# Wide U products in a sparse expert layer: one moving operand of 512 columns, and a sum of two PSUM halves on the vector engine

## The reference

```python
gate = jax.nn.softmax(best, axis=-1)
u = u_tab[idx]
h = jax.nn.gelu(jnp.einsum('bthkd,btd->bthk', u, xi).astype(jnp.float32), approximate=False)
w = (gate * h).astype(xi.dtype)
return jnp.einsum('bthk,bthkd->btd', w, v_tab[idx])
```

## Time and profile before

| | |
|---|---|
| time, median of 3 runs (lowest to highest) | 2306.07 us (2303.71 to 2306.95) |
| profiled execution, its own time | 2305.3 us |
| its span, first to last instruction | 2303.6 us |
| mean granted TensorE clock | 0.99 |
| PE busy | 2247.2 us, 98% of the span |
| DVE busy | 1399.5 us, 61% |
| ACT busy | 1241.2 us, 54% |
| POOL busy | 704.2 us, 31% |
| mean transfer rate | 163 GB/s |

### The profile page before, as it was taken

How to read it: one execution, slowest core, us unless ns; L and a number is a source line. 1 busy time by engine, 2 the same in 40 slices (tenths; PEclk the granted TensorE clock), 3 DMA queues, 4 the chain that set the end, 5 groups by cost and what they waited for, 6 DMA issues and landing times. The chain is left out here.

```text
span 2303.6 us, 38838 instructions
## 1 busy us (share of the span) xinstructions
PE 2247.2 (98%) x15059; PEld 2028.6 (88%) x15059; DVE 1399.5 (61%) x2682; ACT 1241.2 (54%) x2451; POOL 704.2 (31%) x346
## 2 busy tenths in 40 slices
PE   8799999999999999998999999999999999989999
PEld 7689999999888888886999999988888888888998
DVE  6546965566555555564697566655555558346555
ACT  4434467777544444464446777754444444545443
POOL 3205877777200000001487777720000004000000
PEclk9889999999999999999999999999999999999999
DMA  5125555555566666563565555566666656324654
GB/s 165 55 67 164 184 175 165 157 164 159 180 187 188 186 189 186 149 179 99 160 183 175 165 159 163 158 180 185 188 187 190 185 163 223 98 83 157 187 187 147
DMA packets 122535, 375.55 MB, mean 163 GB/s; under 512 B 13024, under 2 KB 17376, under 8 KB 122352
## 3 DMA queue, kind: packets, MB, share of 16 engines
q1 hardware_dynamic: 122352, 373.06, 53.0%
HBM read 371.96 MB, written 1.05 MB: 162 GB/s over the span
## 5 line engine op out<-in xcount | busy, mean ns | idle before, releaser
L248 ACT ACTIVATE hi<-raw 128x1024 fp32r<-128x1024 f32 (+1 forms) x703 | 737.2, 1050 | 429.8 <-PE bank L1249 184.5
L257 DVE TENSOR_TENSOR lo<-raw,hi 128x1024 fp32r<-128x1024 f32 (+2 forms) x443 | 536.9, 1215 | 372.4 <-ACT hi L248 372.0
L257 POOL TENSOR_TENSOR lo<-raw,hi 128x1024 fp32r<-128x1024 f32 x260 | 630.6, 2429 | 252.8 <-ACT hi L248 252.8
L1245 PE MATMUL bank<-xh,hi 128*128 128x256 f32 x2048 | 512.3, 288 | 0.0
L1246 PE MATMUL bank<-xl,hi 128*128 128x256 f32 x2048 | 500.8, 283 | 0.0
L1285 PE MATMUL bank<-hi,pe_mh 128*128 128x512 f32 x1016 | 403.3, 397 | 1.1 <-DVE pe_ml L1528 1.1
L1286 PE MATMUL bank<-hi,pe_ml 128*128 128x512 f32 x1016 | 402.8, 396 | 0.0
L1246 PEld LDWEIGHTS bank<-xl,hi 128*128 128x128 f32 x2048 | 391.8, 191 | 0.1
L1245 PEld LDWEIGHTS bank<-xh,hi 128*128 128x128 f32 x2048 | 390.8, 191 | 0.1
L320 POOL TENSOR_TENSOR rstd<-mean,minus_half 128x1 f32<-128x1 f32 x10 | 5.6, 556 | 976.6 <-DVE mean L327 976.6
L1396 ACT ACTIVATE pe_mh<-pe_hidden 128x256 fp32r<-128x256 f32 x256 | 107.0, 418 | 364.7 <-PE bank L1292 364.7
(11 more groups left out here) (395 smaller groups left out, 3237.7 us busy)
## 6 DMA issues: line engine op xcount, KB each, us to landing
raw<-in_peer_u SPq DMA_DIRECT2D x256, 512.0 KB, 3.6
raw<-in_peer_v SPq DMA_DIRECT2D x256, 512.0 KB, 4.1
raw<-in_w_gate_up SPq DMA_DIRECT2D x44, 512.0 KB, 4.2
raw<-in_w_in SPq DMA_DIRECT2D x34, 512.0 KB, 4.0
raw<-in_gla_w_in SPq DMA_DIRECT2D x24, 512.0 KB, 3.8
raw<-in_w_down SPq DMA_DIRECT2D x22, 512.0 KB, 4.2
raw<-in_w_query SPq DMA_DIRECT2D x16, 512.0 KB, 3.7
raw<-in_mla_w_o SPq DMA_DIRECT2D x8, 512.0 KB, 3.6
```

What stands on the lines that cost most here:

```text
L248: act.activation(k.hi[:, n % RING, 0:x * e], k.raw[:, n % RAW, 0:x * e], ACT.Copy).then_inc(k.hi_done, 1)
L257: eng.tensor_tensor(k.lo[:, n % RING, 0:x * e], k.raw[:, n % RAW, 0:x * e], k.hi[:, n % RING, 0:x * e].bitcast(F32), ALU.subtract).then_in ...
L1245: pe.matmul(ps, hi[:, r, c * P:(c + 1) * P], k.xh[:, c], start=(c == 0), stop=False)
```

## The change

The two activation tensors become one, `xx`, in which the high and the low 256 columns of each piece of the contraction lie side by side; `xh` and `xl` are views of it. From slab 44 on a U slab takes 7 matmuls of 512 columns (high part of the slab by both halves), then the 8 of 256 columns with the low part, and the eighth of 512 last. The bank's left half then holds what was multiplied with `xh`, its right half what was multiplied with `xl`. A new step on DVE, `fold(i)`, adds the two halves into `whole`, a new SBUF tile with two slots. `bend(i)` waits for `fold(i)` and works on `whole`, and `gate_slab(i)` multiplies with `whole`, where it multiplied with the PSUM bank before. PE waits for `folded` of slab i-3 before it writes the bank again.

```diff
-        self.xh = self.sb(ctx, "xh", [P, KD, T], F32R)
-        self.xl = self.sb(ctx, "xl", [P, KD, T], F32R)
+        self.xx = self.sb(ctx, "xx", [P, KD, 2, T], F32R)
+        self.xh, self.xl = self.xx[:, :, 0], self.xx[:, :, 1]
...
-                        if j > LEAD:
-                            pe.wait_ge(gated.sem, gated_before(j))
+                        if j >= LEAD:
+                            pe.wait_ge(folded.sem, folded.at(j - LEAD + 1))
...
-                    for c in range(KD):
-                        pe.matmul(ps, hi[:, r, c * P:(c + 1) * P], k.xh[:, c], start=(c == 0), stop=False)
-                        pe.matmul(ps, hi[:, r, c * P:(c + 1) * P], k.xl[:, c], start=False, stop=False)
+                    if i >= LEAD:
+                        for c in range(KD - 1):
+                            pe.matmul(k.bank[i % 3][:], hi[:, r, c * P:(c + 1) * P],
+                                      k.xx[:, c].rearrange("p s t -> p (s t)"), start=(c == 0), stop=False,
+                                      skip_group_check=True)
+                    else:
+                        for c in range(KD):
+                            pe.matmul(ps, hi[:, r, c * P:(c + 1) * P], k.xh[:, c], start=(c == 0), stop=False)
+                            pe.matmul(ps, hi[:, r, c * P:(c + 1) * P], k.xl[:, c], start=False, stop=False)
...
+                    if i >= LEAD:
+                        last = pe.matmul(k.bank[i % 3][:], hi[:, r, (KD - 1) * P:KD * P],
+                                         k.xx[:, KD - 1].rearrange("p s t -> p (s t)"), start=False, stop=True,
+                                         skip_group_check=True)
                     last.then_inc(k.eaten, 1)
...
-                    act.wait_ge(k.eaten, u0 + i + 1)
+                    if i >= LEAD:
+                        act.wait_ge(folded.sem, folded.at(i - LEAD + 1))
+                    else:
+                        act.wait_ge(k.eaten, u0 + i + 1)
                     ps, cut = first_ps(i), g * GROUP
+                    if i >= LEAD:
+                        ps = whole[:, i % 2]
...
+                def fold(i):
+
+                    dve.wait_ge(k.eaten, u0 + i + 1)
+                    if i >= LEAD + 3:
+                        dve.wait_ge(gated.sem, gated_before(i - 2))
+                    dve.tensor_reduce(whole[:, i % 2], k.bank[i % 3][:].rearrange("p (s t) -> p t s", s=2), AX_X, ALU.add)\
+                       .then_inc(folded.sem, 1)
...
-                    dve.tensor_tensor(hidden[:, i, 0:cut], hidden[:, i, 0:cut], first_ps(i)[:, 0:cut], ALU.mult)\
+                    dve.tensor_tensor(hidden[:, i, 0:cut], hidden[:, i, 0:cut], whole[:, i % 2, 0:cut], ALU.mult)\
                         .then_inc(gated.sem, 1)
...
                 for i in range(LEAD, NK):
+                    fold(i)
```

More of the change, by code:

```diff
@@ L283, in given_squares @@
         k = self.k
-        act.activation(k.xh[:, 0:4].rearrange("p c t -> p (c t)"), k.h[:, 0], ACT.Square, scale=D ** -0.5,
+        act.activation(k.xx[:, 0:2].rearrange("p c s t -> p (c s t)"), k.h[:, 0], ACT.Square, scale=D ** -0.5,
                        accum_out=k.mean[:, 0:1]).then_inc(self.squared.sem, 1)
@@ L296, in given_diagonals @@
         dve.tensor_tensor_reduce(
-            out=k.xl[:, 0:4].rearrange("p c t -> p (c t)"), in0=k.h[:, 1], in1=k.h[:, 1], scale=1.0 / D, scalar=0.0,
+            out=k.xx[:, 2:4].rearrange("p c s t -> p (c s t)"), in0=k.h[:, 1], in1=k.h[:, 1], scale=1.0 / D, scalar=0.0,
             op0=ALU.mult, op1=ALU.add, accum_out=k.mean[:, 1:2]).then_inc(self.summed.sem, 1)
@@ L1132, in peer @@
     names = ("q_act", "q_dve", "zeroed", "keyed", "scored", "s_act", "s_dve", "counted", "raised", "powered",
-             "ranked", "turned", "equal", "hotted", "lowered", "summed", "spread", "applied", "bent", "gated", "m_hi", "m_lo")
+             "ranked", "turned", "equal", "hotted", "lowered", "summed", "spread", "applied", "bent", "gated", "m_hi", "m_lo", "folded")
     (q_act, q_dve, zeroed, keyed, scored, s_act, s_dve, counted, raised, powered, ranked, turned, equal, hotted,
-     lowered, summed, spread, applied, bent, gated, m_hi, m_lo) = (k.sig(f"pe_{x}") for x in names)
+     lowered, summed, spread, applied, bent, gated, m_hi, m_lo, folded) = (k.sig(f"pe_{x}") for x in names)
     hi, lo = k.hi, k.lo
@@ L1147, in peer @@
         count = k.sb(ctx, "pe_count", [P, NK], I32)
+        whole = k.sb(ctx, "pe_whole", [P, 2, T])
         spare = Carver(hidden[:, NK // 2:, :].rearrange("p i t -> p (i t)"))
@@ L1243, in first @@
                     pe.wait_ge(k.hi_done, u0 + i + 1)
-                    for c in range(KD):
-                        pe.matmul(ps, hi[:, r, c * P:(c + 1) * P], k.xh[:, c], start=(c == 0), stop=False)
-                        pe.matmul(ps, hi[:, r, c * P:(c + 1) * P], k.xl[:, c], start=False, stop=False)
+                    if i >= LEAD:
[7 more added lines that the diff above has]
+                            pe.matmul(ps, hi[:, r, c * P:(c + 1) * P], k.xl[:, c], start=False, stop=False)
                     pe.wait_ge(*k.lo_at[u0 + i])
                     for c in range(KD):
-                        last = pe.matmul(ps, lo[:, r, c * P:(c + 1) * P], k.xh[:, c], start=False, stop=(c == KD - 1))
+                        last = pe.matmul(ps, lo[:, r, c * P:(c + 1) * P], k.xh[:, c], start=False,
+                                         stop=(c == KD - 1 and i < LEAD), skip_group_check=(i >= LEAD))
+                    if i >= LEAD:
+                        last = pe.matmul(k.bank[i % 3][:], hi[:, r, (KD - 1) * P:KD * P],
+                                         k.xx[:, KD - 1].rearrange("p s t -> p (s t)"), start=False, stop=True,
+                                         skip_group_check=True)
                     last.then_inc(k.eaten, 1)
@@ L1574, in peer @@
     gated.advance(NK - LEAD - 1)
+    folded.advance(NK - LEAD)
     for x in (equal, hotted, lowered, summed, spread, applied):
@@ L2493, in _ @@
                             act.wait_ge(y_done.sem, y_done.at(m + 1))
-                            act.activation(k.xh[:, 2 * m:2 * m + 2].rearrange("p c t -> p (c t)"), yb[:, m], ACT.Copy)\
+                            act.activation(k.xh[:, 2 * m:2 * m + 2], yb[:, m].rearrange("p (c t) -> p c t", t=T), ACT.Copy)\
                                .then_inc(y_hi.sem, 1)
@@ L2615, in _ @@
                             dve.wait_ge(y_hi.sem, y_hi.at(m + 1))
-                            dve.tensor_tensor(k.xl[:, 2 * m:2 * m + 2].rearrange("p c t -> p (c t)"), yb[:, m],
-                                              k.xh[:, 2 * m:2 * m + 2].bitcast(F32).rearrange("p c t -> p (c t)"),
-                                              ALU.subtract).then_inc(y_lo.sem, 1)
+                            dve.tensor_tensor(k.xl[:, 2 * m:2 * m + 2], yb[:, m].rearrange("p (c t) -> p c t", t=T),
+                                              k.xh[:, 2 * m:2 * m + 2].bitcast(F32), ALU.subtract).then_inc(y_lo.sem, 1)
                 for n, (a, c) in enumerate(END_ORDER):
```

## The result

The changed kernel takes 2343.03 us (median of 4 runs, 2341.58 to 2345.74) against 2304.89 us for the kernel before on the same chip. The ratio is 1.0167, with a 95% interval of 1.0151 to 1.0183: 38 us slower, where 27 were forecast.

What follows compares the result with a forecast made beforehand. PE bounds the kernel, busy 98%; the change makes a ring of DVE, ACT and POOL slower than PE. Losing 20.6 - 3.0 - 4.0 = 13.6 us a layer, 27.2 in two, gives 2333 us, range 2307 to 2355.

Steps and rivals of the forecast that it cites:

- The ring's length: DVE's gate, ACT and POOL waiting on each other in the first U stage: 17.0 to 18.0 us per five slabs.
- step i's one-hots set POOL's end of step i+1: Link through ACT in the first U stage: 6.47 us from DVE's one-hots begun to POOL's end.
- the walk over ten slabs: Gated-stage chain over ten slabs: 7.17 once, x + 4.0 once, x + 6.47 three times, totalling 30.6 + 4x.
- 15.3 + 2x: Gated-stage time for five slabs; x, from POOL's end to the next one-hots, is 0.87 us early, 1.35 late.
- PE's saving: Wide matmuls in U slabs save 0.048 us a slab, 4.0 us a layer, 8.1 in all.
- The slack: Gated stage: the ring may fall 2.97 us behind before PE's sums wait for ACT's low gates; subtracted once a layer.
- DVE catches up before the V stage: After slab 122 there are no more one-hots, so DVE was to recover before the V stage; no loss counted.
- 20.6 - 3.0 - 4.0 = 13.6: Loss per layer in us: ring's excess over PE in 15 fives, less slack, less PE's saving.
- The fold's price: DVE's new reduce from PSUM: taken as 0.60 us from start to start, bounded by 0.33 and 0.87.
- The gate isn't held: Rival, chance 0.12: POOL doesn't delay DVE's gate, PE sets the pace and gains 8.1 us: 2298.
- Held, but hidden: Rival, chance 0.08: gates fall into POOL's gaps often enough for slack and PE's saving to pay: 2302 to 2310.
- The fold is the bound: Rival, chance 0.08: fold of 0.87 us or more overloads DVE, deciding from about 0.67: 2353 or more.

Runs made afterwards that it cites:

- e1: Changed kernel, but `bend` writes GELU back to the slab's PSUM bank and the gate reads it there: 2290.3 us, ratio 0.9939 to the kernel before.
- e4: Changed kernel with POOL's low-part instruction of each U slab cut into two of 512 columns: 2294.8 us, ratio 0.9958 to the kernel before.
- e5: Changed kernel with a second reduce of half the size ahead of each fold: 2377.5 us, ratio 1.0317 to the kernel before.
- e2: e1 with the wide matmuls undone (24 of 256 columns a slab) and the fold kept: 2305.5 us, ratio 0.9997 to the kernel before.
- e3: Kernel before, with only the gate's second input moved to SBUF, no fold or wide matmuls: 2307.6 us, ratio 1.0010 to the kernel before.
- e6: e1 with a second reduce of half the size ahead of each fold: 2291.7 us, ratio 0.9951 to the kernel before.

## Why the prediction was right, and which terms were off

**The mechanism.** POOL's instruction holds the gate, and what stands behind the gate on DVE closes a ring over ACT back to POOL. e1 and e4 take the hold away from either side, and the whole loss of 50 us (25.00 a layer between the stages of e1 and the changed kernel) goes with it. By the rule that the prediction cites from the Trainium skill ("SBUF — State Buffer", section "Who interferes with whom"), the first to issue holds the ports for its whole instruction: the traces agree, in that every gate issued under a POOL instruction ends behind it, by 0.02 us for the smallest to 0.29 for the largest, 0.20 in the rows above.

**The ring's length.** Forecast 17.0 us for five slabs early and 18.0 late; measured 17.17 and 18.28, and 17.64 in the mean of all fifteen fives. The step "step i's one-hots set POOL's end of step i+1" holds (6.46 us). What failed is the walk over ten slabs, in which two chains were to alternate, every gate held. Only one chain is there: of five gates two find POOL idle or at its end. Read in the rows above: POOL, which holds the no-group gate, ends at 499.94 + 2.39 = 502.33, and from there it is 0.72 us to the one-hots at 503.05; 6.46 to POOL's end at 509.51; 1.18 (rest of the gate, apply, fold) to the one-hots at 510.69; then 3.10 of DVE's own work, with a short gate, to those at 513.79; and 6.46 to POOL's end at 520.25. The sum is 17.92, and from fold to fold it is 517.74 - 499.82 = 17.92. The fold stands in this three times, which e5 confirms. That the forecast sum came close in spite of the wrong walk is luck: 15.3 + 2x and the right walk differ by only 0.2 to 0.3 us with a fold of 0.60.

**PE's saving.** "8 x (0.240 - 0.234) = 0.048" took the price of 512 columns from the V stage. In the U stage it is 0.230, and a slab is 2.79. The saving is 6.7 us a layer (e1 against e2), not 4.0. Since PE's speed is also what the ring is compared with, this made the ring's excess larger: 15 x (17.64 - 15.99) = 24.7 us a layer where I had 20.6. A faster PE gains nothing inside a ring that it doesn't set. So this mistake enters the sum twice, 2.7 us too little saved and 15 x (16.16 - 15.99) = 2.6 us too little lost, and nearly cancels, again by luck.

**The slack.** I let 2.97 us be absorbed for good. DVE does fall behind first: its fold starts 0.43 us behind the start of the slab's last wide matmul at slab 44, 1.8 at slab 48, 4.1 at slab 58, 4.4 at slab 98. PE feels nothing until about slab 58. But at slab 123, where the one-hots are over, it is back at 2.5, and only 2.54 - 1.79 = 0.75 us of the 24.7 stay unpaid. That count begins at slab 48. From slab 44 on, where the ring begins, DVE falls behind by 1.36 us more, 26.1 in all; against e1, 24.0 of them have reached PE by slab 123 and 1.05 follow at the door of the V stage, so that about 1 us is absorbed for good, not 3.0. Most of the slack was a loan.

**The door of the V stage.** "DVE catches up before the V stage" was wrong by 1.05 us a layer: POOL still held gates at slabs 122 to 124 (1.47 us for the last, where an unheld one takes 0.42), and the first V matmul waits 1.67 us, where it waits 0.62 in e1 (0.53 in the kernel before):

```profile
591.89 0.50 PE L1297 MATMUL bank<-hi,pe_mh 128*128 128x512 f32 x1 [0.62 <-DVE pe_ml L1553]
```

For one layer: forecast 20.6 - 3.0 - 4.0 = 13.6. Measured 24.7 - 0.75 + 1.05 - 6.68 = 18.3. The 4.7 us a layer between them are 4.1 of the ring, 2.2 of slack and 1.05 of the door, less 2.7 of PE's saving. The fold's price, which I had bounded from 0.33 to 0.87, is 0.60 from start to start (505.54 to 506.13, 0.59), 0.67 long.

**The rivals.** "The gate isn't held" was worth 2298 us; e1 shows what it would have been, 2290. "Held, but hidden" is what e3 shows, without the fold and the wide matmuls. "The fold is the bound" decides, by my text, from 0.67 us on; e6 has 0.93 and loses nothing, so that point was wrong as well: it asks each slab to fit, while only five together must. In e6 DVE falls behind late in the stage, from 0.8 us to 2.3 at slab 118, and is back at 0.8 by slab 123.

## What to carry to other kernels

Before an input of a vector instruction is moved from PSUM to SBUF, look at what GpSimd runs beside it: with two SBUF inputs it waited, in every case here, for the end of a running GpSimd instruction that reads SBUF, however small it was itself (a gate of 20 elements took 1.96 us). The price is not the hold alone but what stands behind it, so walk the ring through all engines and count how often each step is in it. Here GELU written back to PSUM, a change of a few lines, turned a loss of 1.7% into a gain of 0.6%; where the operand must stay in SBUF, cutting the GpSimd instruction in two did nearly the same.

## What the runs showed of the hardware that was not expected

- A matmul of 512 columns of float32r took 0.234 us in the V stage and 0.230 in the U stage of e1, at the same granted clock of 1.00, while 256 columns took 0.120 and 0.119. Place by place, the fifth to seventh wide matmul of a slab in e1 start 0.227 us apart and the eighth, behind the low part, takes 0.233, while in the V stage all start 0.234 apart in the mean. What makes the V stage's slower stays open: it was not tried.
- Two POOL instructions of 512 columns took 2.53 to 2.75 us together, the held gate's turn between them included, where one of 1024 took 2.40. I had not counted on nearly all of the ring's 50 us going for so little more of POOL.
- A held DVE instruction counts as busy. DVE's busy time rose from 1399.5 to 1626.6 us in the changed kernel and is 1503.9 in e1, which does the same work; the gates' own share is 184.4 us there against 47.9 in e1, so over 120 us of what reads as busy is standing still.
